# Turning q, k and y1 with VectorE blocks and SBUF transfers instead of TensorE transposes

## The reference

```python
h = rms_norm(x, norm_g)
q, k, v, z = jnp.split(h @ w_in, 4, axis=-1)          # w_in: 1024 x 8192
q = rope(rms_norm(heads(q), q_norm))
k = rope(rms_norm(heads(k), k_norm))
v = heads(v)
o = moba_attention(q, k, v).transpose(0, 2, 1, 3).reshape(B, S, D_INNER)
return x + (o * jax.nn.silu(z)) @ w_out
```

## Time and profile before

| what | value |
|---|---|
| median of the runs | 431.71 us |
| the profiled execution | 431.68 us |
| its span | 429.9 us |
| TensorE busy | 423.5 us, 99% |
| VectorE busy | 281.4 us, 65% |
| ScalarE busy | 231.0 us, 54% |
| GpSimd busy | 163.1 us, 38% |
| DMA traffic | 75.25 MB, 175 GB/s |

### The profile page before, as it was taken

The page is one execution under the profiler, slowest core; times in us unless marked ns, Lnnn a source line. Parts: engine busy times, 40 slices in busy tenths (PEclk is TensorE's granted clock), DMA queues, the critical chain, the costliest instruction groups (busy, mean ns, idle before and its releaser), DMA issues.

```text
span 429.9 us, 5672 instructions
## 1 busy us (share of the span) xinstructions
PE 423.5 (99%) x2214; PEld 362.7 (84%) x2214; DVE 281.4 (65%) x340; ACT 231.0 (54%) x406; POOL 163.1 (38%) x111
## 2 busy tenths in 40 slices
PE   8999999999999999999999999999999999999997
PEld 8979898988888888888788888888888888888885
DVE  3866898688985544356664798447983579836532
ACT  5745545444554443578447765477654786546310
POOL 0077417267000000089804595055940559300000
PEclk9999999999999999999999999999999999999999
DMA  8987578645455747436833667236672355731002
GB/s 273 386 285 272 195 244 314 214 159 178 167 197 175 217 137 221 123 94 204 295 101 99 186 184 226 91 100 193 196 216 84 99 191 196 246 105 41 2 0 98
DMA packets 38026, 75.25 MB, mean 175 GB/s; under 512 B 1648, under 2 KB 1776, under 8 KB 38000
## 3 DMA queue, kind: packets, MB, share of 16 engines
q1 hardware_dynamic: 37280, 73.83, 52.8%
q10 hardware_dynamic: 720, 1.07, 0.8%
HBM read 73.84 MB, written 1.05 MB: 174 GB/s over the span
## 4 chain that ended last, share of the span: by engine, by line
PE 85%; POOL 7%; DMA 2%; DVE 2%; ACT 1%; SPq 1%; issue 1%; DVEq 0%
PE acc L599 23%; PE acc L601 22%; PE acc L600 22%; PE aux L654 4%; POOL wide L344 3%; PE acc L644 3%; PE acc L643 3%; PE acc L641 3%; DMA raw<-in_w_in_dram 2%; PE aux L738 2%; POOL k_s L337 1%; PE aux L745 1%; SPq L232 1%; PE aux L757 1%; PE aux L756 1%; PE aux L755 1%
## 5 line engine op out<-in xcount | busy, mean ns | idle before, releaser
L836 DVE TENSOR_TENSOR w_lo<-raw,w_hi 128x2048 fp32r<-128x2048 f32 x65 | 165.2, 2548 | 57.6 <-ACT w_hi L367 57.5
L367 ACT ACTIVATE w_hi<-raw 128x2048 fp32r<-128x2048 f32 x64 | 121.9, 1915 | 28.3 <-PE acc L601 21.7
L599 PE MATMUL acc<-w_hi,hT_hi 128*128 128x512 f32 x320 | 127.7, 399 | 1.0 <-DVE w_lo L836 1.0
L601 PE MATMUL acc<-w_hi,hT_lo 128*128 128x512 f32 x320 | 124.9, 390 | 0.0
L600 PE MATMUL acc<-w_lo,hT_hi 128*128 128x512 f32 x320 | 124.6, 389 | 0.0
L601 PEld LDWEIGHTS acc<-w_hi,hT_lo 128*128 128x128 f32 x320 | 60.1, 188 | 13.0
L599 PEld LDWEIGHTS acc<-w_hi,hT_hi 128*128 128x128 f32 x320 | 60.2, 188 | 12.9 <-DVE w_lo L836 1.4
L600 PEld LDWEIGHTS acc<-w_lo,hT_hi 128*128 128x128 f32 x320 | 60.2, 188 | 11.5
L599 PE MATMUL acc<-w_hi,aT_hi 128*128 128x512 f32 x160 | 63.7, 398 | 0.0
L601 PE MATMUL acc<-w_hi,aT_lo 128*128 128x512 f32 x160 | 62.4, 390 | 0.0
L600 PE MATMUL acc<-w_lo,aT_hi 128*128 128x512 f32 x160 | 62.3, 389 | 0.0
(11 more groups left out here) (125 smaller groups left out, 593.7 us busy)
## 6 DMA issues: line engine op xcount, KB each, us to landing
raw<-in_w_in_dram SPq DMA_DIRECT2D x46, 1024.0 KB, 5.5
raw<-in_w_out_dram SPq DMA_DIRECT2D x16, 1024.0 KB, 5.0
raw<-in_w_pool_dram SPq DMA_DIRECT2D x4, 1024.0 KB, 5.5
raw<-in_w_in_dram SPq DMA_DIRECT2D x8, 256.0 KB, 7.4
wide<-in_xT_dram ACTq DMA_DIRECT2D x4, 256.0 KB, 6.6
xs<-in_x_dram SPq DMA_DIRECT2D x1, 1024.0 KB, 7.7
out_dram<-ysb SPq DMA_DIRECT2D x4, 256.0 KB, 2.0
wide<-in_table_dram SPq DMA_DIRECT2D x1, 256.0 KB, 8.9
```

The lines of the kernel that those rows point to most:

```text
L367: act.activation(w_hi[:, slot, :], raw[:, slot, :], ACT.Copy).then_inc(hi_made, 1)
L599: pe.matmul(a, shi, whi, start=first and k == 0, stop=False)
L601: ins = pe.matmul(a, slo, whi, start=False, stop=last and k == GK - 1)
L836: dve.tensor_tensor(w_lo[:, slot, :], raw[:, slot, :], w_hi[:, slot, :].bitcast(F32), ALU.subtract).then_inc(w_split, 1)
```

## The change

1. GpSimd no longer rotates or scales: it makes the powers only, and for q also their negatives (`minus_rstd`), which VectorE had made per head.
2. ScalarE scales k by head and token tile (`scale_k`, eight activations of 128x128) between `w(4)` and `w(5)`.
3. VectorE rotates (`rope`: two products of 128x512, two operations of 128x1024) and turns 32x32 blocks within each quarter of the partitions (`blocks`, one transpose of 128x1024), q after `w(4)`, k after `w(6)`. y1 of the group before is turned in blocks after `w(5)` (`y1_turn`).
4. SP moves the blocks to their quarter: 16 transfers each of 32 partitions by 256 floats (32 KB), from SBUF to SBUF, for q, for y1 (not in group 0) and for k. They stand in SP's stream ahead of the loads of granules 8g+12, 8g+13 and 8g+14.
5. TensorE no longer turns q, k and y1, except the last group's y1. ScalarE no longer copies `qT`, `kT`; it and VectorE split y1 from SBUF instead of PSUM.

```diff
+            def move_blocks(dst, blocks, landed):
+                for b in range(P // Q):
+                    for a in range(P // Q):
+                        sp.dma_start(dst[b * Q:(b + 1) * Q, a * 2 * P:(a + 1) * 2 * P],
+                                     blocks[a * Q:(a + 1) * Q, b * 2 * P:(b + 1) * 2 * P]).then_inc(landed, 16)
+            def move_q(g):
+                sp.wait_ge(qk_blocked[0], g + 1)
+                sp.wait_ge(scores_ready, HPG * g)
+                move_blocks(qkT[:, 0].rearrange("p h s -> p (h s)"), flat(scratch[0]), qkT_landed[0])
+            def move_y1(g):
+                sp.wait_ge(y1_blocked, g + 1)
+                move_blocks(flat(y1), y1_blocks, y1T_landed)
+            for i in range(8 * GROUPS + 8):
+                g, j = divmod(i - 7, 8)
+                if i >= 7 and g < GROUPS:
+                    if j == 5:
+                        move_q(g)
+                    if j == 6 and g > 0:
+                        move_y1(g - 1)
+                    if j == 7:
+                        move_k(g)
...
+            def scale_k(g):
+                act.wait_ge(k_rstd_made, g + 1)
+                for t in range(TT):
+                    for h in range(HPG):
+                        tile = k_s[:, t, h * HEAD_DIM:(h + 1) * HEAD_DIM]
+                        ins = act.activation(tile, tile, ACT.Copy, scale=k_rstd[:, t, h:h + 1])
...
                 w(7)
+                if attend:
+                    y1_hi(g - 1)
                 tanh_z(g, not attend)
-                if attend:
-                    y1_hi(g - 1)
-                qkT_out(g, 1)
...
                 for i in range(2):
-                    pe.wait_ge(qkT_made[i], 2 * (g + 1))
+                    pe.wait_ge(qkT_landed[i], 256 * (g + 1))
...
-                    if j == 6:
-                        turn_qk(g, 0, first)
-                    if j == 7:
-                        if not first:
-                            turn_y1(g - 1, g)
-                        turn_qk(g, 1, first)
...
+            def rope(g, i):
...
+                for a, b in ((0, half), (half, 0)):
+                    tab = rope_tab[:, 2 * i + 1, :, a:a + half].unsqueeze(2).to_broadcast([P, TT, HPG, half])
+                    ins = dve.tensor_tensor(s4[:, :, :, a:a + half], v4[:, :, :, b:b + half], tab, ALU.mult)
+                chain.done(ins)
+                tab = rope_tab[:, 2 * i, :, :].unsqueeze(2).to_broadcast([P, TT, HPG, HEAD_DIM])
+                chain.done(dve.tensor_tensor(v4, v4, tab, ALU.mult))
+                chain.done(dve.tensor_tensor(qk[i], qk[i], scratch[i], ALU.add))
+                order = "p (b i n) -> p n b i" if i == 0 else "p (b n i) -> p n b i"
+                blocks(scratch[i].rearrange("p t n -> p (t n)"), qk[i], order).then_inc(qk_blocked[i], 1)
...
                 w(4)
-                rope_sum(g, 0)
+                rope(g, 0)
                 if attend:
                     head_out(g - 1, 3)
                 w(5)
+                if attend:
+                    y1_turn(g - 1)
                 w(6)
-                rope_sum(g, 1)
+                rope(g, 1)
                 w(7)
```

More of the change, by code:

```diff
@@ L14 @@
 P = 128
+Q = 32
 SEQ = 256
@@ L193, in bass_hybrid_trunk @@
         qk_scaled = sem("qk_scaled")
[L194 to L197, removed]
+        k_rstd_made, k_scaled = sem("k_rstd_made"), sem("k_scaled")
+        qk_blocked = [sem("q_blocked"), sem("k_blocked")]
+        qkT_landed = [sem("qT_landed"), sem("kT_landed")]
+        y1_blocked, y1T_landed = sem("y1_blocked"), sem("y1T_landed")
         scores_ready, bias_made, exp_made = sem("scores_ready"), sem("bias_made"), sem("exp_made")
@@ L203, in bass_hybrid_trunk, with y_tiles @@
         block = ctx.enter_context(nc.Block())
+        def y_tiles(dst, g, t):
+            return dst[:, HPG * g:HPG * (g + 1), t * P:(t + 1) * P].rearrange("p h (a i) -> p h a i", i=Q)
         def product_ready(eng, t, i, n):
@@ L329, in norm_rope @@
                     pool.wait_ge(exp_made, HPG * (g - 1))
-                scaled = pool.tensor_tensor(q_rstd[:, g % 2] if i == 0 else k_rstd[:, :, :], qk_mean[:, i],
-                                            minus_half[:, :].rearrange("p (t h) -> p t h", t=TT), ALU.pow)
+                ins = pool.tensor_tensor(q_rstd[:, g % 2] if i == 0 else k_rstd[:, :, :], qk_mean[:, i],
+                                         minus_half[:, :].rearrange("p (t h) -> p t h", t=TT), ALU.pow)
                 if i == 0:
-                    scaled.then_inc(qk_scaled, 1)
-                else:
[L335 to L349, removed]
+                    chain.done(ins)
+                    pool.tensor_scalar(minus_rstd[:, g % 2], q_rstd[:, g % 2], -1.0, 1.0, ALU.mult,
+                                       ALU.mult).then_inc(qk_scaled, 1)
+                else:
+                    ins.then_inc(k_rstd_made, 1)
             for g in range(GROUPS):
-                norm_rope(g, 0)
-                norm_rope(g, 1)
+                norms(g, 0)
+                norms(g, 1)
         @block.scalar
@@ L482, in qkv_evacuate @@
                 elif which < 2:
-                    act.wait_ge(qk_turned[which], 2 * g)
+                    act.wait_ge(qk_blocked[which], g)
                 else:
@@ L492, in qkv_evacuate @@
                     act.wait_ge(qkv_out[which], TT * (g + 1))
+                    if g > 0:
+                        act.wait_ge(qkT_landed[which], 256 * g)
                     for t in range(TT):
@@ L501, in qkv_evacuate @@
                                    bias=HEAD_DIM * EPS).then_inc(squared[which], 1)
[L503 to L508, removed]
+            def scale_k(g):
[4 more added lines that the diff above has]
+                        ins = act.activation(tile, tile, ACT.Copy, scale=k_rstd[:, t, h:h + 1])
+                ins.then_inc(k_scaled, 1)
             def tanh_z(g, first):
@@ L518, in y1_hi, with y1_hi_last @@
             def y1_hi(g):
+                act.wait_ge(y1T_landed, 256 * (g + 1))
+                for t in range(TT):
+                    act.activation(y_tiles(aT_hi, g, t), y1T[:, :, t].rearrange("p a h i -> p h a i"),
+                                   ACT.Copy).then_inc(y_hi, 1)
+            def y1_hi_last():
                 for b in range(2):
-                    turned_hi(aT_hi, HPG * g + 2 * b, b, (y_turned, 8 + 2 * g + b + 1), y_hi)
+                    turned_hi(aT_hi, HPG * last + 2 * b, b, (y_turned, 8 + b + 1), y_hi)
             def layer1(g, attend):
@@ L544, in layer1 @@
                     probs_out(g - 1, 3)
+                scale_k(g)
                 w(5)
@@ L547, in layer1 @@
                 w(6)
-                qkT_out(g, 0)
                 w(7)
-                tanh_z(g, not attend)
                 if attend:
                     y1_hi(g - 1)
-                qkT_out(g, 1)
+                tanh_z(g, not attend)
             h1_hi(1)
@@ L569, in _ @@
                     probs_out(last, j - 1)
-            y1_hi(last)
+            y1_hi_last()
         @block.tensor
@@ L730, in scores @@
                 for i in range(2):
-                    pe.wait_ge(qkT_made[i], 2 * (g + 1))
-                if h < 2:
-                    pe.wait_ge(y_split, 8 + 2 * g)
+                    pe.wait_ge(qkT_landed[i], 256 * (g + 1))
+                if HPG * g + h < 2:
+                    pe.wait_ge(h_split, 4)
                 else:
@@ L736, in scores @@
                 s = aux[h % 2]
-                pe.matmul(s[:, 0:P], qT[:, h, 0:P], kT[:, h, 0:P], start=True, stop=True)
-                pe.matmul(s[:, P:3 * P], qT[:, h, P:SEQ], kT[:, h, :], start=True, stop=True).then_inc(scores_ready, 1)
+                pe.matmul(s[:, 0:P], qT[:, 0, h, :], kT[:, 0, h], start=True, stop=True)
+                pe.matmul(s[:, P:3 * P], qT[:, 1, h, :], kT[:, :, h], start=True, stop=True).then_inc(scores_ready, 1)
             def turn_probs(g, h):
@@ L758, in values @@
                           stop=True).then_inc(o_ready, 1)
[L760 to L774, removed]
             def attend(g, j):
@@ L816, in y_needed @@
                 if k % 2 == 0:
-                    pe.wait_ge(y_split, 8 + k // 2 + 1)
+                    pe.wait_ge(y_split, 8 + (k // 2 + 1 if k >= HPG * last else 2 * (k // HPG) + 2))
             for j, (half, q) in enumerate(OUT1_ORDER):
@@ L999, in head_out @@
                 dve.wait_ge(o_ready, HPG * g + h + 1)
-                dve.wait_ge(y_turned, 8 + 2 * g)
+                dve.wait_ge(y_split, 8 + 2 * g)
                 for t in range(TT):
@@ L1005, in head_out, with blocks, y1_turn @@
                 ins.then_inc(y1_made, 1)
-            def rope_sum(g, i):
-                dve.wait_ge(rope_parts[i], g + 1)
-                dve.tensor_tensor(qk[i], qk[i], scratch[i], ALU.add).then_inc(roped[i], 1)
+            def blocks(dst, src, order="p (b n i) -> p n b i"):
+                return dve.transpose(dst.rearrange(order, b=P // Q, i=Q),
```

(26 more changed lines are left out.)

39 lines of the change are left out of this document (23 added, 16 removed).

## The result

The changed kernel takes **503.38 us**, the median of four runs (502.73 to 504.02), against 431.73 (four runs): a ratio of 1.165, with a 95% interval of 1.1618 to 1.1682. It is slower by 71.65 us. The forecast was 453.7 in a range of 438 to 474: the direction was right, the size far off, three times too small. The profiled execution took 502.78 us, its span is 501.0.

A forecast was written before the change was run, and what follows sets the result against it. TensorE was taken to bound the kernel, busy 423.5 of 429.9 us. Gain -10.4, new idle +27.3 and clock restarts +5.1 made +22.0 on 431.7: 453.7 us, range 438 to 474.

The forecast's parts named there:

- Where TensorE stands: TensorE in layer 1 has no idle time outside group 0; each removed instruction is won, each new wait costs its full length.
- the 10.4 us of gain: On TensorE, at most: 11 turns of 0.87 us gone, 9.6, plus 0.8 us for k's late turn in group 0.
- the idle time was to be put down to a DMA: Sign: TensorE idle before each group's first score products, put down to a DMA, 4 to 9 us each, four times.
- The path: 50 SP issues in a row delay the next group's first scores; new idle 4.9, 7.0, 7.0, 8.4, sum 27.3 us.
- The price of an issue: On SP, one 32 KB transfer was taken at 0.40 us, with ends 0.35 and 0.51; size hardly matters.
- The block transpose: On VectorE, 128x1024 taken at 1.2 us, bounds 0 and 2.3; with rope 5.0 us for q or k.
- the estimate of 2.5: On VectorE: eight bf16 128x128 transposes at the skill's 311 ns, 2.5 us, putting the sum near the third rival.
- the third rival: On VectorE the block transpose takes two passes, 2.3 us; idle 32.8 us, total 459.2 us; chance 0.12.
- q's strided read: Strided read of qT as TensorE weights in 32 score products: nothing to 6 us, nothing taken.
- The clock: TensorE restarts at its lower clock after the three long idle stretches: 1.7 us each, 5.1; nothing for group 0's 4.9.
- the rival that it stays up: TensorE's clock stays up through the idle stretches, total 448.6 us; chance 0.18.
- Work with cover: No cost expected: ScalarE's scaling (2 us a group), y1's landing wait (up to 3 us if uncovered), SP's later loads.

The follow-up runs named there:

- the rotation alone: Against the kernel before: rotation on VectorE, scaling of k on ScalarE, powers alone on GpSimd, all turns on TensorE, no transfers; 430.93 us (0.998).
- The filled holes: The changed kernel with 84 (group 0: 49) overwritten matmuls ahead of each group's first scores, in TensorE's idle time; 499.88 us (1.1577).
- the kernel without holes: Against the kernel before: only y1 turned by blocks and transfers, q and k rotated by VectorE, scaled by ScalarE, turned by TensorE; 429.81 us (0.9955).
- the first filled run: The changed kernel with 75 (group 0: 45) overwritten matmuls ahead of each group's first scores, in TensorE's idle time; 501.91 us (1.1629).

## Why the prediction was wrong, step by step

**Where TensorE stands.** Right: all its idle time is new and costs in full. Of the 10.4 us of gain the runs confirm two parts by themselves: the rotation alone gave 0.8, three turns 2.6. The other eight turns were not tried alone. One sign was read wrongly: the idle time was to be put down to a DMA, and the view says "issue".

**The path.** Right: q's blocks, then SP's row of 48 moves and two loads, then the landing, then the first scores; the second split, y1's blocks and k's blocks all early. The landing after the last issue was 1.37, taken 1.65. In group 0 the prediction let VectorE's path to k's blocks come last. That holds at 0.40 an issue but not at 0.63: k's blocks were ready at 216.9 (216.0 expected), while SP issued from 207.58 to 229.32, and the scores started at 230.71.

**The price of an issue.** This is the step that failed. The prediction took 0.40 us and bounded it by 0.35 and 0.51 from the earlier trace rows; the moves took 0.63. "The size hardly matters" is true, but every one of those rows has HBM at one end, and these transfers have SBUF at both. The bound from above was no bound for this kind, since no row of the kernel before shares the feature that counts. 0.63 in the same working gives idle times of 18.5, 18.5, 19.9 and, in group 0, where q's blocks at 206.6 and 34 issues now come last, 10.6: sum 67.5, against 69.7 measured, and with the clock lost four times a time of 431.7 - 10.4 + 67.5 + 6.8 = 495.6.

**The block transpose.** Right for k and y1, 1.25 for 1.2, and the estimate of 2.5 beside it is not borne out; wrong for q, 2.27, by its strided output, as the run with side-by-side blocks shows. As SP's row starts at q's blocks, that adds 1.0 to each hole, 4 in all: 499.6. It was the third rival's price, for one tensor of three.

**q's strided read.** Taken at nothing, "nothing to 6": it costs about 3.4 us, by the run with side-by-side blocks. It does not hide behind the product before it.

**The clock.** The mechanism was right, and the rival that it stays up falls. The earlier trace rows gave 1.7 a restart, counted three times; it fell four times. Just behind the four holes (same columns as above):

```profile
230.71:236.00 5.29, 5.29 (x17) 4.39 (x18) 3.10 (x6) 1.10 (x4) 0.00 (x0) 0.67 0.66 195
302.83:308.00 5.17, 5.17 (x17) 4.34 (x18) 3.10 (x6) 1.10 (x4) 0.00 (x0) 0.70 0.66 200
374.72:380.00 5.28, 5.28 (x18) 4.38 (x19) 3.10 (x6) 1.21 (x5) 0.00 (x0) 0.73 0.66 196
446.55:454.00 7.45, 7.45 (x21) 6.01 (x22) 3.10 (x6) 3.01 (x5) 0.00 (x0) 0.59 0.53 180
```

With 0.50 as the low level that is 3.5, 3.1, 2.9 and 6.1 us at it, and a product then starts 0.43 behind the last in place of 0.23, so 0.47 x 15.6 = 7.3 us are lost on TensorE. The price from the start of the kernel came near for three of the four, but the start is not the same reading: there the clock reads 1.00 although the products come at half the pace, here it reads 0.50. The filled holes gave back 3.5 in the medians and 4.0 in the spans (501.0 to 497.0); some issue rows of that run took 0.6 longer, and part of the lost time may have been waited anyway, which no run separates.

Put together for the spans, 429.9 to 501.0: -10.4 + 69.7 + 3.4 + 7.3 = +70.0 of the 71.1 measured. The 1.1 left over is not explained.

**Work with cover.** ScalarE's scaling took 2.4 us a group (2 expected) and was hidden. The loads were never late. y1's landing was not free everywhere: in the hole it cost nothing, but in the kernel without holes its wait on ScalarE held the copy of k's turn back, 1.5 us in all, the kind of queueing that the prediction had named only for tanh and the next split.

## What to carry to other kernels

Price a transfer by issues before bytes, and take the price from a transfer of the same two ends, in a row if it stands in one: sixteen small moves cost their queue 10 us here whatever they carried. A row of issues in an in-order queue is a latency for whoever needs the last one, so such moves suit data that is wanted late (y1: 3.5 us won with the rotation) and not data wanted within a granule or two (k, the last of the row: 70 us of idle time). When the engine at the bound is made to pause, add its restart at the low clock.

## What the runs showed of the hardware that was not expected

- Issuing a transfer from SBUF to SBUF occupies SP for 0.51 us alone and 0.63 in a row; from HBM 0.46 in a row. A 1 MB load from HBM takes 0.37 alone and 0.58 right behind a row of moves. On ScalarE's queue 0.64 in a row; GpSimd's took 8.11 us for sixteen, 0.51 each.
- From SBUF to SBUF the issue time hardly depends on size: 64 bytes and 1 KB per partition, 32 and 128 partitions, all 10.05 to 10.18 us for sixteen.
- VectorE's block transpose of 128x1024 float32 takes 1.24 with blocks written side by side and 2.27 with elements eight apart.
- A TensorE weight load of 128x128 with columns eight apart takes 318 ns in place of 188, and it is not hidden.
- The granted clock fell in mid-program in pauses of 11.6 to 20.3 us, and around short ones not by their length alone: in the run with fewer issues it fell behind pauses of 1.6 and 2.95 us and not behind two of 1.9, in the first filled run it fell at 3.0 and 3.8 and not at 1.6 and 2.0. In the low stretch products stand 0.43 apart.
